# Second block's first two norms and the last norm: per-token columns on TensorE in place of 256-wide rows on VectorE

## The reference, cut to what matters

```python
def rmsnorm(x, g):
    y = x * lax.rsqrt(jnp.mean(x * x, axis=-1, keepdims=True) + 1e-6)
    return y * g

def first_block(x, ...):
    ...
    return rmsnorm(x, final_norm)                        # norm A

def second_block(x, c, ...):                             # x is the output of the first block
    mod = silu(c) @ w_ada + b_ada
    sh1, sc1, gt1, sh2, sc2, gt2 = split(mod, 6)
    h = rmsnorm(x, g_mix) * (1 + sc1) + sh1              # norm B
    proj = h @ w_in                                      # 1024 x 4608, the "win2" product
    ...
    x = x + gt2 * hier_moe(...)
    shf, scf = split(silu(c) @ w_ada_f + b_ada_f, 2)
    return rmsnorm(x, g_final) * (1 + scf) + shf         # norm C, the last
```

## Time and profile before

| | |
|---|---|
| median of 3 runs | 1872.03 us |
| lowest and highest of them | 1859.14 and 1872.08 us |
| the profiled execution's own time | 1854.46 us |
| its span, first to last instruction | 1852.7 us |
| mean granted TensorE clock | 0.965 |
| busy share: PE / DVE / ACT | 93% / 70% / 49% |

### The profile page before, as it was taken

The page is one execution under the profiler, slowest core; times in us unless marked ns, Lnnn a source line. Parts: engine busy times, 40 slices in busy tenths (PEclk is TensorE's granted clock), DMA queues, the critical chain, the costliest instruction groups (busy, mean ns, idle before and its releaser), DMA issues.

```text
span 1852.7 us, 29088 instructions
## 1 busy us (share of the span) xinstructions
PE 1720.3 (93%) x11854; PEld 1543.1 (83%) x11854; DVE 1299.7 (70%) x2300; ACT 899.6 (49%) x1654; POOL 11.1 (1%) x22
## 2 busy tenths in 40 slices
PE   5999998999998999998899997996798889999997
PEld 5999986899998999977899997995697866666664
DVE  6666855778887888776687877757664576666664
ACT  5444635645445544543644444432421566666662
POOL 0000010000000000000000000000000000000000
PEclk9999999999999999997999998998898899999998
DMA  7555432345664665540456652430000448888871
GB/s 313 226 184 192 183 148 92 126 168 231 252 229 182 229 246 225 207 182 1 160 205 250 243 221 106 160 137 23 24 1 31 197 180 335 340 340 337 338 291 64
DMA packets 48518, 351.81 MB, mean 190 GB/s; under 512 B 5504, under 2 KB 5632, under 8 KB 6144
## 3 DMA queue, kind: packets, MB, share of 16 engines
q1 hardware_dynamic: 47952, 348.07, 49.2%
q10 hardware_dynamic: 432, 1.87, 0.2%
HBM read 348.87 MB, written 1.05 MB: 189 GB/s over the span
## 4 chain that ended last, share of the span: by engine, by line
PE 82%; DVE 12%; ACT 3%; issue 1%; DMA 1%; DVEq 0%; ACTq 0%; SPq 0%
PE ps L393 21%; PE ps L394 20%; PE ps L395 20%; PE ps L2659 6%; DVE WL L387 2%; PE ps L1945 1%; PE ps L1925 1%; PE ps L1030 1%; PE ps L1951 1%; PE ps L1835 1%; PE ps L1421 1%; DVE acc L704 1%; DMA ring<-in_w 1%; PE ps L958 1%; PE ps L997 1%
## 5 line engine op out<-in xcount | busy, mean ns | idle before, releaser
L393 PE MATMUL ps<-HH,WH 128*128 128x256 f32 x1696 | 489.0, 288 | 36.9 <-DVE WL L387 23.6
L387 DVE TENSOR_TENSOR WL<-ring,WH 128x512 fp32r<-128x512 f32 x728 | 448.4, 684 | 53.9 <-ACT WH L379 49.9
L394 PE MATMUL ps<-HL,WH 128*128 128x256 f32 x1696 | 484.2, 285 | 0.0
L395 PE MATMUL ps<-HH,WL 128*128 128x256 f32 x1696 | 482.8, 285 | 0.0
L379 ACT ACTIVATE WH<-ring 128x512 fp32r<-128x512 f32 x728 | 391.3, 617 | 97.2 <-PE ps L395 83.3
L393 PEld LDWEIGHTS ps<-HH,WH 128*128 128x128 f32 x1696 | 324.4, 191 | 39.7 <-DVE WL L387 18.2
L394 PEld LDWEIGHTS ps<-HL,WH 128*128 128x128 f32 x1696 | 324.7, 191 | 0.1
L395 PEld LDWEIGHTS ps<-HH,WL 128*128 128x128 f32 x1696 | 324.8, 191 | 0.0
L2611 DVE TENSOR_TENSOR EL<-ring,EH 128x1024 fp32r<-128x1024 f32 x140 | 164.8, 1220 | 73.3 <-ACT EH L2604 73.3
L393 PE MATMUL ps<-AH,WH 128*128 128x256 f32 x704 | 201.4, 286 | 6.9 <-DVE AL L673 6.9
L652 ACT ACTIVATE AF<-AF 128x256 f32<-128x256 f32 x88 | 36.8, 418 | 347.6 <-DVE AF L669 347.6
(11 more groups left out here) (492 smaller groups left out, 2545.8 us busy)
## 6 DMA issues: line engine op xcount, KB each, us to landing
ring<-in_w SPq DMA_DIRECT2D x292, 1024.0 KB, 4.9
AR<-in_w SPq DMA_DIRECT2D x35, 1024.0 KB, 4.8
cols<-in_s SPq DMA_DIRECT2D x1, 2994.0 KB, 12.9
cons<-in_k ACTq DMA_DIRECT2D x1, 1698.0 KB, 13.7
XT<-in_x SPq DMA_DIRECT2D x1, 1024.0 KB, 5.4
out<-SQ SPq DMA_DIRECT2D x4, 256.0 KB, 2.3
cols<-in_s ACTq DMA_DIRECT2D x1, 126.0 KB, 5.6
pos<-in_p ACTq DMA_DIRECT2D x1, 1.0 KB, 7.7
```

Of the source, the lines that this page charges most:

```text
L387: ins = v.tensor_tensor(lo(n)[:, s], ring[:, i % RING, s], hi(n)[:, s].bitcast(F32), ALU.subtract)
L393: pe.matmul(out, ah, bh, start=start, stop=False, skip_group_check=skip)
L394: pe.matmul(out, ah, bl, start=False, stop=False, skip_group_check=skip)
L395: return pe.matmul(out, al, bh, start=False, stop=stop, skip_group_check=skip)
```

## The change

Three things are done differently; what is computed stays the same.

1. **Sums as columns by token.** The squares become the stationary operand, 128 tokens at a time, and the moving operand is a column of ones, and for norms A and B together two columns: ones and nf squared (`on2`). A token's sum then lands in its own partition, and the result for all 256 tokens is 128x2. The squares of XT times nf (L471) go away. Roots, reciprocals and the products between them work on 128x2 tiles (`r1`, `r2`).
2. **The row is made by a product.** VectorE multiplies the identity by r, which gives two diagonal 128x128 matrices (`dve_diag`), and TensorE multiplies ones by these (`pe_row`): every output partition gets the row of r in PSUM.
3. **The element work is divided anew.** ScalarE multiplies XT by the gain (into TMP, or SQ at the end), VectorE multiplies by the row in PSUM two chunks at a time, and ScalarE adds the shift. RS, which norm A's output needs, is copied from a second such row. The table load for the root is moved ahead of the squares, and the gains `gm` and `g12` are formed ahead of the last residual.

```diff
+        def pe_row(pe, q, n, bank):
+            for th in range(2):
+                m = pe.matmul(ps[:, bank, th * 128:th * 128 + 128], KC("ones"), DG[:, n + th, :], start=True, stop=True)
+            m.then_inc(*q.up(p_row))
+        def dve_diag(v, q, n, r):
+            v.tensor_tensor(DG[:, n:n + 2, :], ident.unsqueeze(1).broadcast_to([P, 2, 128]), r.unsqueeze(2).broadcast_to([P, 2, 128]), ALU.mult).then_inc(*q.up(v_sq))
         def pe_two_norms(pe, q):
             q.wait_ge(v_mod, 32)
+            q.wait_ge(v_sq, 20)
             for k in range(8):
-                q.wait_ge(a_sq, 24 + 2 * (k // 2) + 1)
-                m = pe.matmul(ps[:, 7, 0:T], KC("ones"), SQ[:, k, :], start=k == 0, stop=k == 7)
...
-                m = pe.matmul(ps[:, 6, 0:T], KC("ones"), S2[:, k, :], start=k == 0, stop=k == 7)
+                q.wait_ge(a_sq, 24 + k // 2 + 1)
+                for th in range(2):
+                    m = pe.matmul(ps[:, 6 + th, 0:2], SQ[:, k, th * 128:(th + 1) * 128], on2[:, k, :], start=k == 0, stop=k == 7)
             m.then_inc(*q.up(p_ss))
+            q.wait_ge(v_sq, 22)
+            pe_row(pe, q, 0, 5)
+            q.wait_ge(v_sq, 23)
+            pe_row(pe, q, 2, 4)
-        def act_two_norms(act, q, x):
+        def act_two_norms(act, q, x, shift):
+            act.activation(warm, epsc, ACT.Sqrt)
             for i in range(4):
                 q.wait_ge(*x(i))
                 act.activation(SQ[:, 2 * i:2 * i + 2, :], XT[:, 2 * i:2 * i + 2, :], ACT.Square).then_inc(*q.up(a_sq))
-                for k in (2 * i, 2 * i + 1):
-                    ins = act.activation(S2[:, k, :], XT[:, k, :], ACT.Square, scale=C("nf", k, k + 1))
-                ins.then_inc(*q.up(a_sq))
-            act.activation(warm, epsc, ACT.Sqrt)
             q.wait_ge(p_ss, 7)
-            act.activation(RS[:, :], ps[:, 7, 0:T], ACT.Sqrt, scale=1.0 / D, bias=epsc).then_inc(*q.up(a_rms))
+            act.activation(r1, ps[:, 6:8, 0:1].rearrange("p b n -> p (b n)"), ACT.Sqrt, scale=1.0 / D, bias=epsc).then_inc(*q.up(a_rms))
             q.wait_ge(v_sq, 20)
-            act.activation(R2, R2, ACT.Sqrt, scale=1.0 / D, bias=epsc).then_inc(*q.up(a_rms))
+            for i in range(4):
+                for k in (2 * i, 2 * i + 1):
+                    ins = act.activation(TMP[:, k, :], XT[:, k, :], ACT.Copy, scale=g12[:, k:k + 1])
+                ins.then_inc(*q.up(a_sq))
+                if i == 0:
+                    q.wait_ge(v_sq, 21)
+                    act.activation(r2, r2, ACT.Sqrt, scale=1.0 / D, bias=epsc).then_inc(*q.up(a_rms))
             for i in range(4):
                 q.wait_ge(v_xn, i + 1)
+                for k in (2 * i, 2 * i + 1):
+                    ins = act.activation(SQ[:, k, :], SQ[:, k, :], ACT.Identity, bias=shift[:, k:k + 1])
+                ins.then_inc(*q.up(a_sh))
+                q.wait_ge(a_sh, i + 1)
                 act.activation(HH[:, 2 * i:2 * i + 2, :], SQ[:, 2 * i:2 * i + 2, :], ACT.Copy).then_inc(*q.up(a_hh))
...
+            dve_diag(v, q, 0, r2)
+            dve_diag(v, q, 2, r1)
             for i in range(5):
                 if i < 4:
-                    for k in (2 * i, 2 * i + 1):
-                        v.scalar_tensor_tensor(out=SQ[:, k, :], in0=XT[:, k, :], scalar=g12[:, k:k + 1], in1=R2, op0=ALU.mult, op1=ALU.mult).then_inc(*q.up(v_own))
-                        q.own()
-                        ins = v.tensor_scalar(SQ[:, k, :], SQ[:, k, :], shift[:, k:k + 1], None, ALU.add)
-                    ins.then_inc(*q.up(v_xn))
+                    q.wait_ge(a_sq, 28 + i + 1)
+                    q.wait_ge(p_row, 1)
+                    v.tensor_tensor(SQ[:, 2 * i:2 * i + 2, :], TMP[:, 2 * i:2 * i + 2, :], ps[:, 5, 0:T].unsqueeze(1).broadcast_to([P, 2, T]), ALU.mult).then_inc(*q.up(v_xn))
...
+            q.wait_ge(p_row, 2)
+            v.tensor_copy(RS[:, :], ps[:, 4, 0:T]).then_inc(*q.up(v_own))
```

More of the change, by code:

```diff
@@ L420, in act_norm @@
[L420 to L432, removed]
+            q.wait_ge(p_ss, 7)
@@ L442, in dve_norm @@
-                    ins.then_inc(*q.up(v_xn))
[L443 to L446, removed]
-        S2 = AR[:, 0:2048].rearrange("p (k t) -> p k t", k=8)
-        R2 = AR[:, 6144:6400]
-        g12 = small[:, 494:502]
-        def pe_two_norms(pe, q):
-            q.wait_ge(v_mod, 32)
-            for k in range(8):
-                q.wait_ge(a_sq, 24 + 2 * (k // 2) + 1)
-                m = pe.matmul(ps[:, 7, 0:T], KC("ones"), SQ[:, k, :], start=k == 0, stop=k == 7)
-                if k == 7:
-                    m.then_inc(*q.up(p_ss))
-                q.wait_ge(a_sq, 24 + 2 * (k // 2) + 2)
-                m = pe.matmul(ps[:, 6, 0:T], KC("ones"), S2[:, k, :], start=k == 0, stop=k == 7)
-            m.then_inc(*q.up(p_ss))
@@ L506, in dve_two_norms, with pe_last_norm, act_last_norm, dve_last_norm @@
                     v.tensor_tensor(HL[:, j:j + 2, :], SQ[:, j:j + 2, :], HH[:, j:j + 2, :].bitcast(F32), ALU.subtract).then_inc(*q.up(v_hl))
+            q.wait_ge(p_row, 2)
+            v.tensor_copy(RS[:, :], ps[:, 4, 0:T]).then_inc(*q.up(v_own))
+            q.own()
+        def pe_last_norm(pe, q):
+            q.wait_ge(v_oa, PASSES)
+            for k in range(8):
+                q.wait_ge(a_sq, 36 + k // 2 + 1)
+                for th in range(2):
+                    m = pe.matmul(ps[:, 6 + th, 0:1], SQ[:, k, th * 128:(th + 1) * 128], KC("ones", 0, 1), start=k == 0, stop=k == 7)
+            m.then_inc(*q.up(p_ss))
+            q.wait_ge(v_sq, 24)
+            pe_row(pe, q, 0, 5)
+        def act_last_norm(act, q, x, gain, shift):
+            act.activation(warm, epsc, ACT.Sqrt)
+            for i in range(4):
+                q.wait_ge(*x(i))
+                act.activation(SQ[:, 2 * i:2 * i + 2, :], XT[:, 2 * i:2 * i + 2, :], ACT.Square).then_inc(*q.up(a_sq))
+            q.wait_ge(p_ss, 9)
+            act.activation(r1, ps[:, 6:8, 0:1].rearrange("p b n -> p (b n)"), ACT.Sqrt, scale=1.0 / D, bias=epsc).then_inc(*q.up(a_rms))
+            for i in range(4):
+                for k in (2 * i, 2 * i + 1):
+                    ins = act.activation(SQ[:, k, :], XT[:, k, :], ACT.Copy, scale=gain[:, k:k + 1])
+                ins.then_inc(*q.up(a_sq))
+            for i in range(4):
+                q.wait_ge(v_xn, 4 + i + 1)
+                for k in (2 * i, 2 * i + 1):
+                    ins = act.activation(SQ[:, k, :], SQ[:, k, :], ACT.Identity, bias=shift[:, k:k + 1])
+                ins.then_inc(*q.up(a_sh))
+        def dve_last_norm(v, q):
+            q.wait_ge(a_rms, 10)
+            v.reciprocal(r1, r1).then_inc(*q.up(v_own))
+            q.own()
+            dve_diag(v, q, 0, r1)
+            for i in range(4):
+                q.wait_ge(a_sq, 40 + i + 1)
+                q.wait_ge(p_row, 3)
+                x = SQ[:, 2 * i:2 * i + 2, :]
+                v.tensor_tensor(x, x, ps[:, 5, 0:T].unsqueeze(1).broadcast_to([P, 2, T]), ALU.mult).then_inc(*q.up(v_xn))
         def dve_first_norm(v, q):
@@ L2804, in tensor_program @@
             pe_experts(pe, q)
-            pe_norm(pe, q, "final", (v_oa, PASSES))
+            pe_last_norm(pe, q)
         def scalar_program(act):
@@ L2893, in vector_program @@
             q.own()
-            dve_two_norms(v, q, gm[:, 0:8], MOD[:, 0:8])
+            dve_two_gains(v, q, gm[:, 0:8])
+            dve_residual(v, q, "f2_1")
+            dve_two_norms(v, q)
             dve_split(v, q, 161, 162)
```

88 lines of the change are left out of this document (34 added, 54 removed).

## The result

| | before | after |
|---|---|---|
| median of 20 runs each, same chip | 1865.09 us | 1851.32 us |
| lowest and highest | 1856.15 and 1874.22 | 1839.72 and 1863.10 |
| ratio of the times | | 0.993, 95% interval 0.9908 to 0.9952 |
| span and mean clock of the profiled execution | 1852.7, 0.965 | 1857.0, 0.955 |

The kernel became 13 us faster (9 to 17). Forecast was a gain of 8.6 us and 1863.4 us, range 1845 to 1868. The gain, not the absolute time, is fit to be compared with the forecast: the median of before itself is 7 us lower here than in the three runs shown earlier.

What follows compares the result with a forecast made beforehand. The prediction took TensorE's waits for its next dense product as the bound (82% of the wait chain on TensorE). 6.9 us at the first place plus 1.7 at the last norm, 8.6 off 1872.03, gave 1863.4 us, range 1845 to 1868.

Steps and rivals of the forecast that it cites:

- The first place: Norms A and B ahead of win2: a shorter chain would release the split of group 3 6.9 us earlier.
- first root: First place, behind the sixteen narrow sums taken at 3.8 us: the root could start 2.85 us earlier.
- row's product starts: First place, TensorE multiplying ones by the diagonals: due 6.2 us after the sums began, taking 1.1 us at half clock.
- ScalarE, one pair: First place: adding the shift twice (0.91 us) and copying into HH (0.6) takes 1.5 us for each pair.
- TensorE restarts: First place: TensorE begins win2 on the first pair at 1127.85 us, where it began at 1134.16 before.
- split of group 3: ScalarE's split released by the end of win2's group 0: at 1137.8 us, where 1144.69 was read before.
- the delay of full clock: First place: full clock comes 7.9 us after TensorE's restart, as before, so at 1135.75 us.
- The lower bound by the experts' stage: That stage ran 5.8 us at half clock; with this delay the first place would end 0.9 us earlier.
- The last norm: Norm at the program's end: root stays in place, then ScalarE's sixteen instructions bound it; 1.7 us gained.
- Dearer additions on ScalarE: Rival: ScalarE's shift additions don't overlap, 0.47 us more per pair; gain only 4.5 us, 1867.5 us; chance 0.10.
- Given back behind the first place: Rival: following groups wait for splits or the ring, leaving only the last norm's 1.7 us, 1870.3 us; chance 0.06.
- The clock's rival: Rival: narrow sums drop TensorE's clock sooner; full clock 40 us later would give 1880.6 us, slower; chance 0.04.

Runs made afterwards that it cites:

- e6: Changed kernel with the first place's sixteen narrow sums made a second time into unused columns; first sum to group 3's split took 24.92 us, against 18.53.
- e3: Changed kernel with unused dense matmuls in TensorE's two idle stretches at the first place (16 and 24); first sum to group 3's split 18.90 us, against 18.53.
- e5: Kernel before with 76 unused dense matmuls in TensorE's idle stretch behind the first place's sums; ratio to before 0.9981.
- e7: Changed kernel with its sums, roots and row kept, but VectorE's old two instructions per chunk again, at both places; ratio to before 0.995.
- e11: Kernel before, with TensorE's first win2 matmul waiting for the second pair too; first sum to group 3's split 27.37 us, against 27.17.
- e1: Kernel before with only the first place changed, the last norm left old; ratio to before 0.9946.
- e2: Kernel before with only the last norm changed, the first place left old; ratio to before 0.9982.
- e9: Changed kernel, reordered only: four gain products ahead of the root at both places, VectorE adding the last norm's last pair's shift; ratio to before 0.9956.
- e10: e7 with TensorE's first win2 matmul waiting for the second pair too; first sum to group 3's split 21.15 us, against 22.42.
- e4: Changed kernel with the second row's product moved behind the first group of 48 matmuls; first sum to group 3's split 18.53 us, unchanged.
- e8: Changed kernel with unused dense matmuls at both places and a new order on ScalarE and VectorE; ratio to before 0.9951.

## Why the prediction was right

**The size.** Forecast 8.6 us as 6.9 and 1.7; the stretches give 8.64 and 1.99, together 10.6, and the ratio 9 to 17 us. So the gain was forecast somewhat too low: 8.6 lies just under that interval, and the 10.6 lies just above the 4.5 to 10 us by which the costs were said to bound it. The mechanism came true, each part in its place. The absolute time owes something to luck: 1851.32 is 12.1 us under the 1863.4 forecast, 6.9 of it because the median of before came out lower than in its first three runs, and the range held because it had been drawn wide for such a change of level.

**The first place, step by step.** Offsets, predicted and measured:

| step | predicted | measured |
|---|---|---|
| first root | +3.85 | +3.67 |
| second root done | +5.35 | +4.91 |
| row's product starts | +6.2 | +5.82 |
| first multiplication | +7.3 | +7.15 |
| ScalarE, one pair | 1.5 us | 1.46 us |
| TensorE restarts | +10.35 | +10.31 |
| last pair starts | +14.85 | +14.60 |
| full clock | +18.25 | +14.46 |
| split of group 3 | +20.3 | +18.53 |

Up to the last pair no step is off by more than 0.45 us. The row's product was rightly put at half clock, for the clock had fallen at +4.2; from its start to the first multiplication it took 1.33 us in place of 1.1. The reason given, the time since the last dense matmul, holds in after and in e6, where the clock fell amid narrow matmuls without a pause; e3, where it fell 0.9 us after dense matmuls had begun again, shows that it isn't the whole.

Of the 8.64 us, 6.33 are the earlier restart and 0.97 the two waits between the pairs that are gone. Eighteen of group 0's 48 matmuls began at half clock in place of 29; eleven by 0.09 us are about 1.0, an estimate from the two prices. The remaining 0.3 is not assigned. So the earlier rise is worth about an eighth of the gain in F.

**The mis-sized term** is the delay of full clock: "Before, full clock came 7.9 us after the restart. The same delay gives 1135.75". It came 4.2 us after. That is 3.8 us of half clock less than forecast, at 0.43 each 1.6 us of the 1.77 that are missing between +20.3 and +18.53. The lower bound by the experts' stage (5.8 us, worth 0.9) was not low enough either. The delay after a restart isn't a constant: it read 4.1 to 10.0 us in the table above.

**The last norm.** Sums in time for the root at the same place, the table load without effect, and ScalarE alone as bound, all as said. The first product by the gain began 0.16 us after the root in place of 0.30, and the sixteen instructions took 6.47 us in place of 6.65. Hence 6.63 us from the root in place of 6.95, which accounts for the 0.29 us by which this gain was forecast too low. The clock fell after the root, so the last sums lost nothing:

```profile
1842.31:1847.60 5.29, 4.93 (x44) 4.76 (x42) 3.22 (x8) 2.52 (x4) 0.00 (x0) 1.00 0.01 3
1847.73:1848.73 1.00, 0.03 (x1) 0.03 (x1) 0.59 (x2) 1.00 (x4) 0.00 (x0) 0.64 0.00 0
```

**The rule weighed.** The Trainium skill (TensorE: Matmul & The Clock Gate, section LDWEIGHTS) gave 107 ns for a load of 128 columns; by it the prediction estimated 3.4 us for the 32 records, against 3.8 taken. At full clock the trace agrees with the page: the 32 records took 3.48 us in the chain, 109 ns each. From first start to last end they covered 3.63 us, between the two terms.

**The rivals.** Dearer additions on ScalarE: no, two take 0.91 us and overlap like the scaled copies. Given back behind the first place: no, the next split starts 5.70 us later as at full rate, and M did not grow in after. The clock's rival: the clock does fall earlier, +4.2 against +11.0, but also comes back 10.2 us earlier; it turned out as a help.

**M, and what stays open.** M holds the same code in all kernels, yet it differs, and it goes with the time at half clock within it: 68.3 us in before, e5, e7 and e11 (M 690.7 to 692.7), 64.8 in after, e1, e2, e3, e6, e9 and e10 (M 689.7 to 691.2), 61.4 in e4 and e8 (M 689.2 and 689.4). The timelines agree up to some 110 us behind F and part where the clock falls and rises at other instants. After has 3.4 us less at half clock in M than before, and M is 1.3 us shorter, as 0.39 us for each would have it. With this the stretches sum to 11.9 us, near the ratio's 13. They also fit the 10.0 us at equal time at half clock: the change takes 3.4 us at half clock off F and 3.4 off M and adds 1.7 in L, 5.1 in all, worth 2.0 us by the same slope. Not found was why the clock's instants in M move with the first place (e2, with the old first place, has the 64.8), nor what makes the time at half clock differ from one execution of the same kernel to the next.

## What to carry to other kernels

Price a norm between dense products by three things apart: the chain of engines up to TensorE's restart, the pace of the pairs behind it, and where the clock falls and rises. The first two came out of durations of similar instructions to within half a microsecond. For the third, read several places of the trace rather than one, and give the range what they span. A later start without interruptions once beat an earlier one (e10, by 1.3 us) and once lost to it (e11, by 0.2), and filling gaps with spare matmuls lost where the gap held a short product that others wait for (e3, e8). When runs of one kernel lie on different levels, compare them at equal time at half clock as well: here that gives 10.0 us plus or minus 0.6 beside the ratio's 9 to 17, and what the change saves in time at half clock is counted apart. Per-token numbers as columns paid where two wide reciprocals were in the chain, 4.75 us or more, and paid nothing where only one was; there the gain came from sharing the element work between two engines.

## What the runs showed of the hardware that was not expected

- Narrow plain fp32 matmuls (two moving columns, 128 columns of weights) cost 0.22 us each at full clock and 0.40 at half. The clock fell 3.9 to 4.4 us after the first of them in each of the nine kernels that have them at the first place, in e6 in the midst of an unbroken row of them. With sums of 256 columns it fell at +11.0, 3.9 us after their end. The last norm repeats it: 3.9 to 4.6 us after the first narrow sum in eight kernels (3.4 in e8, which has dense matmuls just ahead), 3.8 to 4.2 us after the end of the 256-column sums in the four that have those.
- The clock fell at +4.4 in e3 although dense work had resumed 0.9 us earlier, and fell in e5 after two pairs of 0.97 us of matmuls with waits of 1.19 behind each.
- At the first place it took 3.4, 10.2, 13.7 or 17.1 us from fall to rise, in 13 readings; elsewhere in the same traces 6.8 is as common as 3.4.
- One microsecond at half clock cost the whole program 0.39 us in 148 timed runs and 0.41 in the thirteen traces up to the first sum, and the time at half clock accounts for nearly all of the spread of one kernel's runs.
